# Where TensorE spreads the second token half's inverse deviations: behind the norm, or inside the matmuls that follow it

## What is computed

```
h = rmsnorm(x, norm_mix_g[i]) * (1 + sc1) + sh1
y = pool_mixer(h)                       # layer 0
y = sgu_mixer(h)                        # layer 1: u, v = split(gelu(h @ w_in)); v = layernorm(v); ...
x = x + g1 * y
h = rmsnorm(x, norm_mlp_g[i]) * (1 + sc2) + sh2
x = x + g2 * (square(relu(h @ w1)) @ w2)
...
rmsnorm: x * rsqrt(mean(x*x over channels) + 1e-6) * gain
```

## Time and profile before

| | |
|---|---|
| time, median of 3 runs | 2611.22 us (2610.31 to 2612.18) |
| the profiled execution's own time | 2611.85 us |
| its span in the trace | 2610.1 us |
| PE busy | 2553.2 us (98%) |
| PEld busy | 2080.1 us (80%) |
| DVE busy | 1383.7 us (53%) |
| ACT busy | 894.6 us (34%) |
| POOL busy | 283.5 us (11%) |

### The profile page before, as it was taken

One profiled execution on the slowest core, in us unless ns is written; L12 is line 12 of the kernel. 1 busy time (PEld: TensorE's weight loads), 2 busy tenths in 40 slices (PEclk: granted clock), 3 DMA queues, 4 the chain that ended last, 5 costly groups with the idle time before them and its releaser, 6 DMA issues.

```text
span 2610.1 us, 33394 instructions
## 1 busy us (share of the span) xinstructions
PE 2553.2 (98%) x12000; PEld 2080.1 (80%) x12000; DVE 1383.7 (53%) x2136; ACT 894.6 (34%) x1394; POOL 283.5 (11%) x275
## 2 busy tenths in 40 slices
PE   8999999999999999999999999999999999998998
PEld 4578888888888788888888888888888897886677
DVE  5864555545454543443434343434652225998873
ACT  2442222222223332333222222222422125887751
POOL 1200000000002000100000000000010002557631
PEclk9899999999999999999999999999999999999999
DMA  8532231322211810321111111110325463445621
GB/s 294 195 113 81 81 110 67 109 84 95 98 64 41 234 45 1 113 82 64 48 48 48 48 48 48 48 48 0 113 82 147 145 174 87 98 109 152 158 71 65
DMA packets 178577, 245.18 MB, mean 94 GB/s; under 512 B 55857, under 2 KB 132785, under 8 KB 178481
## 3 DMA queue, kind: packets, MB, share of 16 engines
q1 hardware_dynamic: 178480, 243.92, 30.1%
HBM read 210.33 MB, written 39.58 MB: 96 GB/s over the span
## 4 chain that ended last, share of the span: by engine, by line
PE 90%; DVE 4%; issue 2%; POOL 2%; ACT 1%; DMA 0%; DVEq 0%; POOLq 0%; SPq 0%; ACTq 0%
PE banks L1907 24%; PE banks L1909 24%; PE banks L1908 24%; PE banks L2398 3%; PE banks L2380 3%; PE banks L1997 2%; PE banks L2368 1%; PE banks L2367 1%; PE banks L1938 1%; PE banks L2165 1%; PE banks L2167 1%; PE banks L2166 1%; DVE acc L1385 1%; POOL probs L939 1%; PE banks L2350 1%
## 5 line engine op out<-in xcount | busy, mean ns | idle before, releaser
L1907 PE MATMUL banks<-Hhi,Whi 128*128 128x512 f32 x1696 | 669.3, 395 | 6.7 <-ACT TB L1154 5.0
L1909 PE MATMUL banks<-Hhi,Wlo 128*128 128x512 f32 x1696 | 662.0, 390 | 0.0
L1908 PE MATMUL banks<-Hlo,Whi 128*128 128x512 f32 x1696 | 662.0, 390 | 0.0
L1600 DVE SCALAR_TENSOR_TENSOR X<-banks,mod,X 128x512 f32<-128x512 f32 x512 | 380.9, 749 | 207.0 <-PE banks L1909 204.3
L1907 PE MATMUL banks<-Mhi,Whi 128*128 128x512 f32 x1024 | 400.0, 391 | 0.0
L1909 PE MATMUL banks<-Mhi,Wlo 128*128 128x512 f32 x1024 | 398.5, 389 | 0.0
L1908 PE MATMUL banks<-Mlo,Whi 128*128 128x512 f32 x1024 | 398.4, 389 | 0.0
L1907 PEld LDWEIGHTS banks<-Hhi,Whi 128*128 128x128 f32 x1696 | 319.8, 189 | 76.9 <-ACT TB L1154 5.8
L1908 PEld LDWEIGHTS banks<-Hlo,Whi 128*128 128x128 f32 x1696 | 319.9, 189 | 67.9 <-issue 2.4
L1909 PEld LDWEIGHTS banks<-Hhi,Wlo 128*128 128x128 f32 x1696 | 319.5, 188 | 67.6
L1022 ACT ACTIVATE Whi<-stage 128x2048 fp32r<-128x2048 f32 x89 | 169.9, 1909 | 540.9 <-PE banks L1909 540.9
(11 more groups left out here) (203 smaller groups left out, 2820.9 us busy)
## 6 DMA issues: line engine op xcount, KB each, us to landing
stage<-w SPq DMA_DIRECT2D x64, 1024.0 KB, 5.6
stage<-ada_w SPq DMA_DIRECT2D x48, 1024.0 KB, 5.4
stage<-w_in SPq DMA_DIRECT2D x13, 1024.0 KB, 6.3
stage<-sgu_in SPq DMA_DIRECT2D x8, 1024.0 KB, 7.2
x_saved<-X SPq DMA_DIRECT2D x16, 512.0 KB, 2.6
QS<-q_heads SPq DMA_DIRECT2D x32, 256.0 KB, 4.3
KH<-k_heads SPq DMA_DIRECT2D x32, 256.0 KB, 5.3
KL<-k_heads SPq DMA_DIRECT2D x32, 256.0 KB, 6.4
```

Source lines behind the costliest of these rows:

```text
L1600: nc.vector.scalar_tensor_tensor(out=X[:, k, half(hf)], in0=Dn[:, i % D_BANKS, :], scalar=gate[:, k:k + 1], in1=X[:, k, half(hf)], op0=ALU ...
L1907: nc.tensor.matmul(out_bank, whi, xhi, start=start, stop=False)
L1908: nc.tensor.matmul(out_bank, whi, xlo, start=False, stop=False)
L1909: return nc.tensor.matmul(out_bank, wlo, xhi, start=False, stop=stop)
```

## The change

In norms 1, 2 and 3 the spread of half 1 is taken out of the norm. In up it comes behind channel tile k = 2 of half 0, in the values in front of the first matmul with k = 3. Because bank 1 still holds the sums of half 1 until the reciprocal has been taken, the first matmuls may no longer write it: bank 5 takes its place for output tile 1 of the first up and for token tile 1 of the values, and bank 1 goes where bank 5 was. Norm 4 only calls the new function and does what it did.

```
     def value_bank(c, t):
-        return PS_ALL[:, ((0, 1, 3, 4, 5, 6, 7, 2), (0, 1, 3, 4, 5, 2, 0, 1))[c][t], :]
+        return PS_ALL[:, ((0, 5, 3, 4, 1, 6, 7, 2), (0, 5, 3, 4, 1, 2, 0, 5))[c][t], :]
     def up_bank(i, first):
-        return PS_ALL[:, (0, 1, 3, 4)[i] if first else i % A_BANKS, :]
+        return PS_ALL[:, (0, 5, 3, 4)[i] if first else i % A_BANKS, :]
...
     def norm(T, which, order):
...
                 if order != "down":
                     pe.wait_ge(tb_ready, T("b"))
                     spread(T, 0, B7)
-                if which != 4:
-                    spread(T, 1, Dn[:, 0, :])
+
+            def second_spread(T):
+                T.add(n=-2)
+                spread(T, 1, Dn[:, 0, :])
+                T.add(n=2)
...
     def up(T, par, first=False):
                             for f in range(FT):
                                 tile_of_up(T, hf, f, k, True)
+                            if hf == 0 and k == 2:
+                                second_spread(T)
...
     def value_part(T, c, kh, tokens, slot, k_first=False):
                 for t, k in ...
+                    if k_first and (t, k) == (0, 3):
+                        second_spread(T)
...
     def first_heads(T):
                         if hf == 0 and k == 2:
-                            T.add(n=-2)
-                            spread(T, 1, Dn[:, 0, :])
-                            T.add(n=2)
+                            second_spread(T)
```

## The result

The changed kernel takes 2616.84 us (median of 14 runs, 2614.98 to 2618.67), the kernel before 2611.56 us (14 runs, 2610.20 to 2613.36). The ratio is 1.0018 with a 95% interval of 1.0011 to 1.0026, that is 2.9 to 6.8 us slower. The forecast was 2613.6 us with a range up to 2617.0, so the direction and the range held, the range by 0.16 us only. The size is about double the +2.4 us of the sum, and 2616.84 us lies above the 2615.0 us that the sum gives with every term at its upper end. The profiled execution of the changed kernel took 2614.98 us, the lowest of its 14, and its span is 2613.2 us.

What follows compares the result with a forecast made beforehand. TensorE, busy 98% of the span, was taken as the bound, so edits pay only at its stops. Terms 0.8 + 0.4 + 1.2 = +2.4 us on the 2611.22 median gave 2613.6 us, range 2609.6 to 2617.0.

Steps and rivals of the forecast that it cites:

- the +2.4 us of the sum: Whole kernel: terms of norms 1, 2 and 3, 0.8 + 0.4 + 1.2; with terms at their ends +1.0 to +3.8.
- rival (a): Norm 2: clock falls before the values start, rises 5.8 us behind; term +3.3, total +5.3, 2616.5 us; chance 0.14.
- Norm 1, taken +0.8: Norm 1: the spread behind 18 matmuls makes NB(8) and TensorE's later restart 0 to 1.6 us late; +0.8 taken.
- the middle between two restarts: Norm 1: clock rises at about 127.6 as before, or 5.8 us behind the restart, at 130.9; +0.8 taken between.
- Norm 2, taken +0.4: Norm 2: values start 3.1 us sooner, but the lead is lost waiting for VectorE's late Hlo; term +0.4 us.
- The queue part of the sum: Norm 2: spread behind 36 matmuls, so VectorE's NB(8) stands still 4.1 us and delays its queue; TensorE waits for Hlo(8).
- If the clock stays up this comes back too: Norm 2, start of the values: the 0.99 us lost before at half clock is regained if the clock stays full.
- Norm 3, taken +1.2: Norm 3: up starts 0.44 us earlier, the spread costs 0.80, plus clock loss: +0.6 to +1.8, middle +1.2 taken.
- No VectorE wait follows there that would absorb a late TensorE: Norm 3: nothing behind it hides TensorE's delay, so the spread's 0.80 us counts in the term.
- Banks and weights: New banks cost nothing; norm 2's second weight split moves to 877.3, still 2.0 us ahead of its use.
- (b): Norm 2: TensorE's lead is kept, VectorE not late; term -3.3, total -2.7, 2608.5 us; chance 0.07.
- (c): Whole kernel: no visible change, the spread being hidden also at norm 3, 2611.2 us; chance 0.12.

Runs made afterwards that it cites:

- e2: Against the kernel before, only norms 1 and 3 have the half 1 spread inside up, norm 2 as before: 2615.29 us, before 2611.18, ratio 1.0013.
- e11: The changed kernel run once more, unaltered, for a second profile and time, against the kernel before: 2616.40 us, before 2611.32, ratio 1.0018.
- e5: The changed kernel with three unused float32 matmuls in each of TensorE's waits at norms 1 to 3: 2612.13 us, kernel before 2611.84, ratio 1.0007.
- e3: Against the kernel before, only norm 2's spread moved, ahead of k = 1 of the values, behind 12 matmuls: 2609.64 us, before 2611.18, ratio 0.9991.
- e1: Against the kernel before, only norm 2's spread moved, ahead of k = 3 as in the changed kernel: 2615.58 us, before 2611.18, ratio 1.0012.
- e7: As e3, plus three unused matmuls ahead of norm 2's sums, one behind norms 1 and 3's half 0 spreads: 2609.24 us, before 2611.84, ratio 0.9992.
- e4: Against the kernel before, only PSUM banks 1 and 5 exchanged, all spreads where they stood: 2611.87 us, before 2611.18, ratio 1.0003.
- e8: Against the kernel before, only norm 3 has the half 1 spread inside up: 2613.13 us, before 2611.84, ratio 1.0003.
- e6: Against the kernel before, only norm 2's spread moved, ahead of k = 2 of the values, behind 24 matmuls: 2613.29 us, before 2611.84, ratio 1.0006.

## Why the prediction was right, and where its size was off

**Direction and kind.** The three places, the late NB(8) of norm 2, TensorE's pauses at token tile 4 (forecast 1.7 and three of 0.6, measured 1.39 and three of about 0.35 in the timeline, as its modelled ends shorten them), the late restart of norm 1 and the spread in norm 3 all came as told. That the total stayed inside the range is in part luck: it lies above the sum with all terms at their upper ends, in the part of the range that was there for rival (a). The values started at 853.11 (forecast 853.1).

**Norm 1, taken +0.8, measured +1.66, 1.31 and in e2 1.18.** The mechanism held, and the size lay in the upper half of the stated 0 to 1.6, once just over its end. The step that failed is the middle between two restarts: the clock rose 5.9 us behind the restart in the profile after (124.75 to about 130.6), 5.1 in e11 and 4.9 in e2, nearer the upper of the two rows than the lower. With TensorE kept at work (e5) the term is 0.10, and with the spread where it was a rise as late costs nothing (e3). So the term needs both, the slow clock and the place behind 18 matmuls.

**Norm 2, taken +0.4, measured +2.05 (2.10 in e1) and 1.12.** The queue part of the sum stands as far as it can be seen alone: NB(8) waited 3.99 us in e11 where 4.1 was worked out, and with the clock kept up (e5) B is 1.20 longer, 0.7 of it the filling's own delay, which leaves 0.5. What failed is the assumption under it, "If the clock stays up this comes back too". The sum had no price for a fall; I had it only as a rival, in the form of a fall ahead of the restart. It fell 1.2 us behind the restart and cost 1.7 us, or later, in the pauses at token tile 4, a place that the prediction had no price for, and cost 0.7 (1.12 less the forecast 0.4).

**Norm 3, taken +1.2, measured +1.02, 0.73, 0.74 and 2.36.** The first three lie in the lower half of the stated 0.6 to 1.8, the middle taken being 1.2. The 2.36 has a longer stretch at 1.2 GHz in it. One reading under the term was wrong: "No VectorE wait follows there that would absorb a late TensorE" holds only while the clock is down. At full clock a wait for ScalarE follows, 1.07 us in e7, and the moved spread costs nothing (C 44.64 in e5 and in e7). With 6.8 us at 1.2 GHz, C is 45.50 to 45.81 with the spread in the norm and 46.26 to 46.55 with it inside.

**Banks and weights.** As forecast, nothing: e4 shows it for the banks in the three stretches. The second half of the weights was split at 876.67 + 2.29 = 879.0, ahead of its use about 881.1, so still covered, by 2 us.

**The rivals.** (a) came in a milder form, with 1.7 us of the 2.9 it priced. (b) does not hold where the spread stands, and e3 shows that it would with the spread ahead of k = 1. (c) falls by e8 at the clock of before, and would hold at full clock, by e5 and e7.

**The sum.** The terms as measured are 4.73 and 4.79 us in two profiles; the times differ by 5.3 us (2.9 to 6.8) and 5.1 (2.4 to 7.1). Of the 4.73, e5 gives back 1.56 at norm 1, 0.85 at norm 2 (net of the 0.7 it costs there) and 1.91 at norm 3, where before's own half-clock loss goes too. So most of the loss appears only where the clock is down, though the clock alone doesn't make it: the late rise of e3 cost nothing with the spread in its old place.

The medians of e1 and e2 lie 2 us above what their stretches give, and that of e6 2.1 us. Their profiles show where such time can lie: at 1.2 GHz in places that no experiment touched. e1 is 1.22 us longer between A and B, with the clock down from 838 to 845, and 1.42 us longer behind C, with the clock down from 1869 to 1872. e2 is 1.35 us longer between A and B, e6 1.55 us behind C, and e4, the banks alone, 4.57 us behind C. The kernel before also took from 2609.80 to 2616.71 us beside e1 to e4. One profile each can't say whether these stretches have a cause in the change, and that stays open.

## What to carry to other kernels

Work that starts earlier is worth nothing if what it pushes back feeds the second half: count the matmuls ahead of the moved instruction, and compare their time with the moment at which the consumer asks for its result. Here 12 matmuls gave 3.1 us at this place and 36 lost 2.1, of which the clock accounts for about 1.6. And an instruction that stands in a wait may be holding TensorE's clock up: with nothing added there, the clock at norm 1 rose 6.4 to 7.5 us behind the reciprocal of half 1 in the three profiles with the spread moved, and 3.1 to 6.4 in the eight with it in place. So price a move out of a wait at both clocks, for the restart and for every stretch in which the engine will then work in pieces. A wait that the trace doesn't show at one clock may be there at the other, as at norm 3.

## What was not expected of the hardware

- The clock fell to 1.2 GHz while TensorE was in full work: in the changed kernel at 854.3, 1.2 us behind the restart of the values, and for 3.4 us. Ahead of the restart TensorE had a wait of 1.56 us and the sums of squares.
- It also fell in e11 at 871, where TensorE had three matmuls of 0.23 us for each 1.33 us. At the same place and pace it did not fall in the first profile of the changed kernel, in e1 or in e5.
- Three float32 matmuls of 128x512 in each wait, about 2.7 us of them, left it at 2.4 GHz through norms 2 and 3 in the one profile of e5. In e7 one of them, 1.0 us, was enough at norm 3. The eleven profiles without added matmuls in that wait have 3.4 to 10.2 us at 1.2 GHz there.
